# The turn of x at a block boundary, a last row by token tile, and a start behind two loads instead of five

## The reference

```python
x = x + 0.5 * swiglu(rmsnorm(x, ffn1_norm), wg, wu, wd)      # d_ff = 2816
x = x + mixer(rmsnorm(x, mix_norm) @ w_in) @ w_out           # attention and a gated recurrence
x = x + 0.5 * swiglu(rmsnorm(x, ffn2_norm), wg2, wu2, wd2)
```

## Time and profile before

| | |
|---|---|
| median of 3 runs | 2074.51 us |
| the profiled execution, its own time | 2076.41 us |
| its span, first to last instruction | 2074.6 us |
| mean granted TensorE clock | 0.996 |
| TensorE busy | 2033.2 us, 98% |
| VectorE busy | 1307.5 us, 63% |
| ScalarE busy | 1057.0 us, 51% |

### The profile page before, as it was taken

How to read it: one execution, slowest core, us unless ns; L and a number is a source line. 1 busy time by engine, 2 the same in 40 slices (tenths; PEclk the granted TensorE clock), 3 DMA queues, 4 the chain that set the end, 5 groups by cost and what they waited for, 6 DMA issues and landing times.

```text
span 2074.6 us, 26738 instructions
## 1 busy us (share of the span) xinstructions
PE 2033.2 (98%) x11144; PEld 1703.0 (82%) x11144; DVE 1307.5 (63%) x1532; ACT 1057.0 (51%) x1278; POOL 54.9 (3%) x72
## 2 busy tenths in 40 slices
PE   7999999999999999999999999999999999999998
PEld 5888888888888887888788898788888889888886
DVE  5655876555655696655565569765556556976554
ACT  4445576444544567544544455654454445565443
POOL 3100004000000000000000000000000000000000
PEclk9999999999999999999999999999999999999999
DMA  9654337555555443555355544355545554435551
GB/s 284 215 185 180 143 123 197 183 189 194 179 187 184 162 143 125 196 182 186 139 203 185 192 151 145 121 183 183 182 168 199 193 191 144 147 118 193 183 188 56
DMA packets 52217, 357.81 MB, mean 172 GB/s; under 512 B 6592, under 2 KB 7008, under 8 KB 9600
## 3 DMA queue, kind: packets, MB, share of 16 engines
q1 hardware_dynamic: 48960, 350.25, 47.5%
q0 software_dynamic: 2416, 5.51, 1.4%
q10 hardware_dynamic: 720, 0.34, 0.1%
HBM read 355.02 MB, written 1.05 MB: 172 GB/s over the span
## 4 chain that ended last, share of the span: by engine, by line
PE 86%; DVE 7%; ACT 3%; DVEq 2%; issue 1%; ACTq 0%; DMA 0%
PE bank L361 80%; DVE w_lo L1093 2%; PE bank L466 2%; DVE arena L1187 1%; PE bank L406 1%; ACT w_hi L751 1%; PE bank L603 1%; PE bank L522 1%; DVEq L1268 0%; DMA cos_sin<-positions 0%; PE bank L589 0%; DVE arena L1272 0%; PE bank L547 0%; PE bank L568 0%; ACT arena L941 0%
## 5 line engine op out<-in xcount | busy, mean ns | idle before, releaser
L1093 DVE TENSOR_TENSOR w_lo<-raw,w_hi 128x2048 fp32r<-128x2048 f32 x332 | 762.0, 2296 | 393.1 <-ACT w_hi L751 392.8
L751 ACT ACTIVATE w_hi<-raw 128x2048 fp32r<-128x2048 f32 x332 | 634.2, 1910 | 258.1 <-PE bank L361 248.6
L361 PE MATMUL bank<-w_hi,h_hi 128*128 128x512 f32 x1536 | 611.5, 398 | 7.1 <-DVE w_lo L1093 4.0
L361 PE MATMUL bank<-w_hi,h_lo 128*128 128x512 f32 x1536 | 600.7, 391 | 0.0
L361 PE MATMUL bank<-w_lo,h_hi 128*128 128x512 f32 x1536 | 600.5, 391 | 0.0
L361 PEld LDWEIGHTS bank<-w_hi,h_hi 128*128 128x128 f32 x1536 | 289.6, 189 | 68.7 <-DVE w_lo L1093 7.5
L361 PEld LDWEIGHTS bank<-w_hi,h_lo 128*128 128x128 f32 x1536 | 289.5, 188 | 61.9
L361 PEld LDWEIGHTS bank<-w_lo,h_hi 128*128 128x128 f32 x1536 | 290.0, 189 | 56.6
L361 PE MATMUL bank<-w_hi,act_hi 128*128 128x512 f32 x832 | 328.3, 395 | 1.8 <-DVE act_lo L1409 1.6
L361 PE MATMUL bank<-w_hi,act_lo 128*128 128x512 f32 x832 | 324.3, 390 | 0.0
L361 PE MATMUL bank<-w_lo,act_hi 128*128 128x512 f32 x832 | 324.0, 389 | 0.0
(11 more groups left out here) (195 smaller groups left out, 1454.7 us busy)
## 6 DMA issues: line engine op xcount, KB each, us to landing
raw<-stream SPq DMA_DIRECT2D x332, 1024.0 KB, 4.8
arena<-rpb POOLq DMA_DIRECT2D x32, 96.0 KB, 9.3
x<-xt SPq DMA_DIRECT2D x4, 256.0 KB, 7.1
arena<-final_gain POOLq DMA_DIRECT2D x2, 512.0 KB, 4.1
out<-x SPq DMA_DIRECT2D x4, 256.0 KB, 2.8
arena<-c_level POOLq DMA_DIRECT2D x1, 384.0 KB, 3.3
arena<-code_w POOLq DMA_DIRECT2D x2, 128.0 KB, 3.5
arena<-c_att POOLq DMA_DIRECT2D x1, 256.0 KB, 4.6
```

The lines of the kernel that those rows point to most:

```text
L361: last = mm(o, a, r, start=start and n == 0, stop=stop and n == len(pairs) - 1)
L751: fn(w_hi[u % SLOTS][:, :], raw[u % RAW][:, :], ACT.Copy).then_inc(hi_done, 1)
L1093: tt(w_lo[u % SLOTS][:, :], raw[u % RAW][:, :], w_hi[u % SLOTS][:, :].bitcast(F32), ALU.subtract).then_inc(lo_done, 1)
```

## The change

**Start.** The first wait is for `square` and `par_all` alone; the other three loads are issued behind ScalarE's table load, with a semaphore of their own on which VectorE's first `tables` step waits. `enter` gets 16 more transposes, of the identity into a bank that nothing reads. `params` gets 8 more columns (PN 36 to 44), the final gain.

**Boundary.** `following` is now set for block 0's last FFN too, so TensorE turns its raw result inside the last row. The gain used on the turned values is `entry_gain`, final gain times FFN gain, made in the third `tables` step. ScalarE makes two roots: the first, of the raw x, into `rms_final`; then VectorE multiplies x in place, as before, and squares of the normed x give `rms`, which is multiplied by `rms_final` per token tile.

**End.** The last row goes through the pieces in the order 0, 2, 1, 3, and squares, root, multiplication and store go by token tile, the first tile (pieces 0 and 2) ahead of the second.

```diff
+LAST_ORDER = (0, 2, 1, 3)
-PN = 36
+PN = 44
+        def turn_gain(b, L, j, k):
+            if (b, L, j) == (1, 0, 0):
+                return entry_gain[:, k:k + 1]
+            return gain(b, L, ("ffn1", "mix", "ffn2")[j], k)
...
-            for i in range(4):
-                wait_x(sp, 14, i)
+            for at, i in enumerate(LAST_ORDER):
+                sp.wait_ge(y_ready, at + 1)
                 sp.dma_start(piece(out, i), piece(x, i)).then_inc(stored, 16)
...
-                for i in range(4):
+                for i in LAST_ORDER if u == ALL_UNITS - 1 else range(4):
...
             def enter(v):
                 for i in range(3):
                     wait_x(pe, v, i)
                     turn(None, x, i // 2, i % 2)
+                for _ in range(16):
+                    nc.tensor.transpose(PD[3][:, 0:P], ident, ident)
...
-                            wait_x(pe, v, 3)
+                            wait_x(pe, v - (v == x_no(1, 0, 0)), 3)
...
-                following = x_no(b, L, 1) if j == 0 else x_no(b, L, 3) if L + 1 < LAYERS else None
+                following = x_no(b, L, 1) if j == 0 else x_no(b, L, 3) if (b, L) != (1, LAYERS - 1) else None
...
-                enter(x_no(b, 0, 0))
+                if b == 0:
+                    enter(x_no(b, 0, 0))
...
-            def root(n):
+            def root(n, dst=rms):
                 act.wait_ge(ms_ready, n + 1)
-                fn(rms[:, :], msum[:, :], ACT.Ln, bias=eps[:, :])
+                fn(dst[:, :], msum[:, :], ACT.Ln, bias=eps[:, :])
                 act.drain()
-                fn(rms[:, :], rms[:, :], ACT.Exp, scale=-0.5)
+                fn(dst[:, :], dst[:, :], ACT.Exp, scale=-0.5)
+                if n == x_no(1, 0, 0):
+                    act.drain()
+                    for t in range(2):
+                        fn(rms[:, t:t + 1], rms[:, t:t + 1], ACT.Copy, scale=rms_final[:, t:t + 1])
                 act.drain().then_inc(rms_ready, 1)
...
-                squares(v, [0, 1])
+                entry = (b, L, j) == (1, 0, 0)
+                squares(v - entry, [0, 1])
                 turned_hi(b, L, 2 * j, [0, 1])
-                squares(v, [2, 3])
+                squares(v - entry, [2, 3])
                 turned_hi(b, L, 2 * j, [2, 3])
+                if entry:
+                    root(v - 1, rms_final)
+                    split(use_of("front", 1))
+                    squares(v, [0, 1, 2, 3])
...
                 root(x_no(b, L, 2 * j))
-                split(use_of("front", 1))
+                if not entry:
+                    split(use_of("front", 1))
                 table(SIGMOID_SET)
...
-            first = [(square...), (par_all...), (freq...), (lb...), (cos_sin...)]
+            first = [(square...), (par_all...)]
+            later = [(freq...), (lb...), (cos_sin...)]
             for dst, src in first:
                 act.dma_start(dst, src).then_inc(first_loaded, 16)
             table(EXP_LN_SET)
+            for dst, src in later:
+                act.dma_start(dst, src).then_inc(table_loaded, 16)
...
-                squares(x_no(b, LAYERS, 0), [0, 1, 2, 3])
-                root(x_no(b, LAYERS, 0))
+            n = x_no(1, LAYERS, 0)
+            for at, i in enumerate(LAST_ORDER):
+                wait_x(act, n, at)
+                fn(h..., piece(x, i), ACT.Square, scale=1.0 / 32, accum_out=ssq[:, i // 2, i % 2:i % 2 + 1])
+                if at % 2:
+                    t = i % 2
+                    act.drain().then_inc(sq_done, 1)
+                    act.wait_ge(ms_ready, n + t + 1)
+                    fn(rms[:, t:t + 1], msum[:, t:t + 1], ACT.Ln, bias=eps[:, :])
+                    act.drain()
+                    fn(rms[:, t:t + 1], rms[:, t:t + 1], ACT.Exp, scale=-0.5)
+                    act.drain().then_inc(rms_ready, 1)
...
-                if v > 0 and not (L == 0 and j == 0):
+                if v > 0:
                     update(nn - 1, (0.5, 1.0)[j], [0, 1, 2])
                     turned_lo(b, L, 2 * j, [0])
                     update(nn - 1, (0.5, 1.0)[j], [3])
                     turned_lo(b, L, 2 * j, [1])
+                    if entry:
+                        mean_square(v - 1)
                     split(use_of("back", 0))
                     turned_lo(b, L, 2 * j, [2, 3])
+                    if entry:
+                        dve.wait_ge(fgain_loaded, 16)
+                        dve.wait_ge(rms_ready, v)
+                        for i in range(4):
+                            stt(piece(x, i), piece(x, i), rms_final[:, i % 2:i % 2 + 1], fgain[...], ALU.mult, ALU.mult).then_inc(x_ready, 1)
+                        split(use_of("front", 1))
                     mean_square(v)
...
-                split(use_of("front", 1))
+                if not entry:
+                    split(use_of("front", 1))
                 split(use_of("front", 0) + SLOTS)
                 dve.wait_ge(rms_ready, v + 1)
                 gated(0)
...
+            def last_norm(t):
+                dve.wait_ge(sq_done, n + t + 1)
+                tt(msum[:, t:t + 1], ssq[:, 0, t:t + 1], ssq[:, 1, t:t + 1], ALU.add).then_inc(ms_ready, 1)
+                dve.wait_ge(rms_ready, n + t + 1)
+                for half in range(2):
+                    i = 2 * half + t
+                    stt(piece(x, i), piece(x, i), rms[:, t:t + 1], fgain[...], ALU.mult, ALU.mult).then_inc(y_ready, 1)
+            for at in range(3):
+                last_update(at)
+            last_norm(0)
+            last_update(3)
+            last_norm(1)
```

More of the change, by code:

```diff
@@ L57 @@
 ALL_UNITS = LAYERS * sum(LAYER_UNITS)
-PCOLS = {"ffn1": (0, 8), "mix": (8, 8), "ffn2": (16, 8), "ogain": (24, 4), "rgain": (28, 4), "bias": (32, 4)}
-PN = 36
+PCOLS = {"ffn1": (0, 8), "mix": (8, 8), "ffn2": (16, 8), "ogain": (24, 4), "rgain": (28, 4), "bias": (32, 4), "final": (36, 8)}
+PN = 44
 def col_source(b, name):
@@ L1044, in mixing @@
                         split(mix_use(b, L, i + 3))
-            first = [(square[:, :, :], c_square[:, 0:2, :]), (par_all[:, :, :], params), (freq[:, :], c_freq), (lb[:, :, :], lower),
+            first = [(square[:, :, :], c_square[:, 0:2, :]), (par_all[:, :, :], params)]
+            later = [(freq[:, :], c_freq), (lb[:, :, :], lower),
                      (cos_sin[:, 0, :].bitcast(I32), bass.AP(tensor=positions.tensor, offset=0, ap=[[0, P], [1, T]]))]
-            assert len(first) == N_FIRST
+            assert len(first) == N_FIRST and len(later) == N_TABLES
             for dst, src in first:
@@ L1109, in turned_lo @@
                         k = 2 * i + c
-                        ins = stt(h_lo[:, k, :], XB[i][:, c * T:(c + 1) * T], gain(b, L, ("ffn1", "mix", "ffn2")[j], k),
+                        ins = stt(h_lo[:, k, :], XB[i][:, c * T:(c + 1) * T], turn_gain(b, L, j, k),
                                   h_hi[:, k, :].bitcast(F32), ALU.mult, ALU.subtract)
@@ L1605, in tables @@
                     dve.wait_ge(trig_ready, 1)
+                    tt(entry_gain[:, :], par_all[:, LAYERS, PCOLS["ffn1"][0]:PCOLS["ffn1"][0] + KC], par_all[:, 0, PCOLS["final"][0]:PCOLS["final"][0] + KC], ALU.mult)
                     ts(lb_all[:, :, 0, :], lb_all[:, :, 0, :], float(40 * np.log(2.0)), None, ALU.subtract)
@@ L1616, in _, with last_update @@
                     ffn(b, L, 1)
-                nn, n = norm_no(b, LAYERS, 0), x_no(b, LAYERS, 0)
-                update(nn - 1, 0.5, [0, 1, 2, 3])
-                mean_square(n)
-                dve.wait_ge(fgain_loaded, 16 * b + 16)
-                dve.wait_ge(rms_ready, n + 1)
-                for i in range(4):
-                    stt(piece(x, i), piece(x, i), rms[:, i % 2:i % 2 + 1], fgain[:, (i // 2) * 512:(i // 2) * 512 + 512], ALU.mult, ALU.mult)\
-                        .then_inc(x_ready, 1)
-N_FIRST, N_CONSTS = 5, 5
+            nn, n = norm_no(1, LAYERS, 0), x_no(1, LAYERS, 0)
+            dve.wait_ge(fgain_loaded, 32)
+            def last_update(at):
+                i = LAST_ORDER[at]
+                if at == 3:
+                    dve.wait_ge(used, last_row(nn - 1) + 1)
+                else:
+                    dve.wait_ge(acc_done, 3 * (nn - 1) + at + 1)
+                stt(piece(x, i), PD[i][:, :], 0.5, piece(x, i), ALU.mult, ALU.add).then_inc(x_ready, 1)
+            def last_norm(t):
[4 more added lines that the diff above has]
+                    i = 2 * half + t
+                    stt(piece(x, i), piece(x, i), rms[:, t:t + 1], fgain[:, half * 512:half * 512 + 512], ALU.mult, ALU.mult).then_inc(y_ready, 1)
+            for at in range(3):
[3 more added lines that the diff above has]
+            last_norm(1)
+N_FIRST, N_TABLES, N_CONSTS = 2, 3, 5
 SIN_SET = 9
@@ L1743 @@
             else:
-                cols += [per_part(i["hgrn_out_norm_2"][L])] * 2 + [per_part(i["hgrn_out_norm_2"][L])]
+                cols += [per_part(i["hgrn_out_norm_2"][L])] * 3
+            cols += [per_part(i["final_norm" + tail])]
             pars.append(np.concatenate(cols, 1))
```

11 lines of the change are left out of this document (10 added, 1 removed).

## The result

| | before | changed |
|---|---|---|
| median of 4 runs each, on one chip | 2075.21 us (2074.14 to 2076.01) | 2064.61 us (2064.53 to 2065.4) |
| ratio of the times, 95% interval | | 0.9949, 0.9937 to 0.9961 |
| the profiled execution, its own time | 2076.41 us | 2064.69 us |
| its span | 2074.6 us | 2062.9 us |
| mean granted TensorE clock | 0.996 | 0.998 |

A forecast was written before the change was run, and what follows sets the result against it. TensorE, 86% of the chain of waits, was taken as the bound. Gains of 6.2 (boundary), 5.0 (start) and 0.0 (end) sum to 11.2 us, subtracted from 2074.51 for 2063.3 us, range 2060.6 to 2066.8.

The forecast's parts named there:

- The start: Kernel start: unit 1 begins at 21.1 instead of 26.09 us, a gain of 5.0 us (bounds 2.9 and 6.6).
- the three moved loads: Kernel start: issued behind the table load, some 1.3 us later than today, with enough cover until use at 40 us.
- The boundary: Between the blocks: 8.2 us of idle and slow clock go, a 2.0 us stall comes, net gain 6.2 us.
- the new stall: First turn_act of block 1: TensorE waits 2.0 us for the gating (bounds 1.6 and 2.6), without a slow clock.
- the wait of 2.76 us at 1779: A stall in the kernel before with granted clock at 1.00, used to charge no slow clock to the boundary's stall.
- the 10.2 us at half clock: Old block boundary: a stretch at granted clock 0.50, begun while TensorE stood idle, counted as part of the removed 8.2 us.
- The table load: Boundary, ScalarE: costs 1.29 us by the profile row; by the Trainium skill's page 2.66, making the boundary's gain 4.8.
- The end: Kernel end: last multiplication some 0.15 us later, stores 2.6 instead of 2.8; gain 0.0 us (bounds -0.4 and +0.5).
- the split by tiles: Kernel end: takes 1.3 us of multiplications off, paid for by a fourth update 1.5 us later behind the first norm.
- The sum: Whole kernel: 6.2 + 5.0 + 0.0 = 11.2 us gained, giving span 2063.4 and time 2063.3 us.
- drift: Rival, behind the boundary: a short slow stretch elsewhere may come or go, 1.7 us either way; chance 0.05.
- slower: Rival, block 1's FFN: the clock falls behind the stall and stays low, +16.5 - 11.2, 2079.8 us; chance 0.02.

The follow-up runs named there:

- e4: The changed kernel without the sixteen transposes of the identity; median 2065.81 us, ratio 0.995 to the kernel before.
- e1: The kernel before with only the start's edits (two loads awaited, three issued later, sixteen transposes); median 2070.68 us, ratio 0.9974.
- e11: The changed kernel, but with the first wait for all five loads again; median 2068.62 us, ratio 0.9963 to the kernel before.
- e2: The kernel before with only the boundary's edits; median 2070.8 us, ratio 0.9972.
- e5: The changed kernel with ScalarE's split of a later weight unit moved ahead of the second root at the boundary; median 2063.26 us, ratio 0.9941 to the kernel before.
- e3: The kernel before with only the end's edits (piece order 0, 2, 1, 3, norm and store by token tile); median 2075.35 us, ratio 0.9995.
- e6: The changed kernel with the fourth update ahead of the first tile's multiplications at the end; median 2063.39 us, ratio 0.9942 to the kernel before.
- e9: The changed kernel with one more table load ahead of the sigmoid's at the boundary; median 2067.22 us, ratio 0.9962 to the kernel before.
- e7: The changed kernel with unit 1 split ahead of the last two turned tiles, front 1 ahead of the root, first FFN only; median 2063.5 us, ratio 0.9942.
- e10: The changed kernel with two more table loads written at the boundary, only one more in the trace; median 2066.01 us, ratio 0.9956 to the kernel before.

## Why the prediction was right

**The start, 5.0 forecast, 5.07 measured.** First split 8.23 (8.1), first product 13.40 (13.5), from there to unit 1 7.62 (7.55), TensorE's wait ahead of unit 1 1.44 (1.7). The first split came out within 0.13 us because the bound, `par_all`'s landing, was read from a row of its own. From the first product to ScalarE's last turned tile (15.27) it took 1.87 us (1.8), and from there to unit 1, ScalarE's and VectorE's work, 5.75 (5.75). The clock did rise in the sixteen transposes (e4 shows that it takes them), but that it rose early enough there is in part luck: in e1 and e11 it did not, and 0.7 us were lost. One step was wrong and cost nothing: I had the three moved loads issued behind the running table load, 1.3 us later; in the changed kernel they go out at 1.69, 2.14 and 3.11, the first two while the load runs from 1.66 to 2.94, and `cos_sin` 0.11 us later than before.

**The boundary, 6.2 forecast, 6.23 measured.** The chain of e2 and of the changed kernel has the forecast's links, and the new stall is 1.78 us (2.0); Exp, the two copies and their drains, for which there was no row, took 0.84 us (0.8). Its cause, ScalarE's order, is shown by e5. That the stall brings no slow clock came true in all seven traces that have it at 1.8 us, but the reason given for it, the wait of 2.76 us at 1779 behind which the clock was at 1.00, does not carry. At the same place in the changed kernel the wait is shorter, and the granted clock fell some 1.8 us after the end of TensorE's last work (1767.56), while it still waited. PE, then a window, of the changed kernel:

```profile
1769.98 0.80 PE L372 MATMUL bank<-w_hi,h_hi 128*128 128x512 f32 x1 [2.42 <-DVE w_lo L1130]
```

```profile
1769.40:1772.80 3.40, 2.82 (x7) 2.24 (x8) 3.40 (x4) 0.61 (x1) 0.00 (x0) 0.50 0.48 140
```

In e3, e4, e5 and e6 too the clock is at half when this wait, 2.41 us there, ends. It cost nothing here: from that product to the next transposes of the mixer it is 7.01 us, and 6.99 in the kernel before at full clock, where TensorE stood waiting for VectorE in the last 1.17 of them.

What was not right either is how I thought of the 10.2 us at half clock. They look like part of what is removed. In e1 the old boundary has the sixteen transposes as well, and the clock is back much sooner:

```profile
1024.40:1027.80 3.40, 3.40 (x18) 3.40 (x17) 1.91 (x5) 2.36 (x8) 0.00 (x0) 0.50 0.00 0
1027.80:1036.20 8.40, 7.85 (x38) 6.19 (x37) 5.06 (x7) 5.12 (x8) 0.00 (x0) 1.00 0.07 8
```

Only 3.4 us are slow, yet the boundary is 26.91 us long against 27.02. The transposes held the first product of block 1, which came 8.79 us behind the last of block 0 instead of 7.11. From there to the product behind `turn_act(0)` it took 18.12 us instead of 19.91, with a new wait of 0.55 for `w_lo`. In the kernel before the first 5.7 us of that stretch are at half clock, and in e1 none are. So the full clock was worth 1.8 us there, where TensorE alone would have gained 2.8. The sum did not suffer, for it was made from the whole distance between two products against that of an ordinary change, and not from the clock. How much of the 6.23 is the clock's alone can't be separated by these runs.

**The table load.** The next activation starts 1.29 us after the load's start (1031.44 to 1032.73), and two loads take 2.57 in e9. By the Trainium skill, ScalarE: Activation LUTs, section "What ACT_TABLE_LOAD costs", there would be a drain of about 1.38 us more at each switch to another set. No run here shows it; by that figure the stall would have been, as an estimate, 3.2 us instead of 1.78.

**The end, 0.0 forecast, 0.17 gained.** The fourth update came 1.4 us later (1.5), the last multiplication ended at the same distance (forecast 0.15 later), the stores took 2.6 instead of 2.8 (2.6). e3 can't be told from no change. e6 shows the forecast's sentence that the split by tiles is paid for by the fourth update: put ahead, it gives 1.3 us back.

**The sum.** 5.07 - 0.20 + 6.23 + 0.45 + 0.17 = 11.72 against 11.2. The 0.45 is no work of the change. In the stretch behind the boundary all other traces but e9's, e3's with the old start and boundary among them (1014.87), lie at 1014.8 to 1015.0, that of before at 1015.4. It is of the kind that I had as the rival "drift", priced at 1.7; without it the traces give 11.3 against 11.2.

**A rival's working.** In "slower", 22.4 us at 1.2 GHz are called four units of weights. A unit is 24 products, 5.5 us at 0.23 each and 10.3 at the slow 0.43, so it is about two units, and 33 us are about three. The price in us is not touched.

**The base.** The weak step of the final number is none of these. I took 11.2 from the median of three runs, 2074.51; from the profiled execution's 2076.41 it would have been 2065.2, and 2064.6 was measured, between the two. The kernel before ran from 2073.0 to 2078.9 us in the experiments' comparisons and e3 from 2072.4 to 2078.1, both with the wait for five loads; e1, with two, from 2070.4 to 2071.6 and the changed kernel from 2064.4 to 2065.4. e2, with five, ran from 2068.0 to 2072.5. The landing of `cos_sin`, 8.7 to 11.3 us in the profiles of these kernels, is long enough to make such a spread, and its absence from the wait fits the changed kernel's narrow one. But e11, which waits for it again, spread by 1.5 only, and e7, which doesn't, by 3.7. So this is possible and not shown.

## What to carry to other kernels

For an edit that removes a wait, work out the distance between two fixed instructions on the bound engine before and after, from a place where the kernel already runs the new order, rather than adding up idle time and slow clock: those overlap with what is late next, here with ScalarE's and VectorE's lists. Don't take one wait behind which the clock stayed up as a proof that a shorter one is safe; price both outcomes. Work split into tiles so that its first part can start early gains nothing if the first part's slow last step stands ahead of the operation that the second part waits for; and a long operation with slack on the engine that makes a stall belongs ahead of the short chain, in the engine's idle time. At a start, wait for the fewest loads, and put first those that land in a steady time.

## What the runs showed of the hardware

- A load's time from issue to landing at the start depends on its kind. Over the fourteen traces `square` took 5.4 to 5.8 us, `par_all` 6.6 to 7.0, `x` (median of four) 6.8 to 7.3, and `cos_sin`, one row read to all 128 partitions, 8.4 to 11.3.
- Sixteen transposes of 128 x 128 straight behind twelve took 2.02 to 3.62 us in ten traces, and 2.28 and 2.90 in two profiles of the same program: the sooner the granted clock rose, the shorter they were, and in the two longest (3.56 and 3.62) the products behind them were the first at full pitch.
- One program by its instruction counts, built twice (e9 and e10): during a wait of 3.08 us the granted clock fell to half for 3.4 us, behind one of 3.11 us it stayed; medians 2067.2 and 2066.0 over 4 runs each.
- At one place of the second block the clock stayed at 1.00 behind a wait of 2.76 us in the kernel before and fell to 0.50 during one of 2.42 us in the changed kernel.
- 3.4 us at half clock cost 1.54 us in e9, and nothing at that place (7.01 us against 6.99), where another wait was due.
- DMAs on ScalarE's queue were issued while its table load ran (1.69 and 2.14, load 1.66 to 2.94).
- Two equal table loads in a row took 2.57 us; three table loads in a row in the source (e10, two equal ones and that of the sigmoid) left two in the trace.
